# Where ScalarE's gates stand between the roots of a norm, and when the gated branch's preparation begins

## What is computed

```python
u = _rms_norm(h, norm_mix_pre[l])
(a_q, a_k, a_v, b_q, b_k, b_v, b_r, b_g, c_qa, c_kva, c_kr,
 d_q, d_k, d_v, gate_logits) = jnp.split(u @ w_in[l], offsets, axis=-1)
o_a = _diff_attention(...)          # branch a, ends in a norm over each head
o_b = _gla(...)                     # branch b: gated linear attention, ends in a norm over each head
o_c = _mla(...)                     # branch c, begins with norms of its latents
o_d = _window_gqa(...)              # branch d
branches = jnp.stack([o_a, o_b, o_c, o_d], axis=2)
gates = jax.nn.sigmoid(gate_logits.reshape(bsz, T, N_BRANCH, D_MODEL))
merged = jnp.sum(jnp.einsum('btnw,nwd->btnd', branches, w_branch[l]) * gates, axis=2)
h = h + _rms_norm(merged @ w_out[l], norm_mix_post[l])
```

## Time and profile before

| | |
|---|---|
| median of three runs | 2257.65 us (2256.54 to 2262.7) |
| the profiled execution: its time | 2256.57 us |
| its span | 2254.8 us |
| TensorE's granted clock over the span | 0.99 |
| weight chunks (instructions of L1653, and of L2077) | 650 |
| table loads of L1646, L1750, L1758 | 22, 2, 12 |

### The profile page before, as it was taken

One profiled execution on the slowest core, in us unless ns is written; L12 is line 12 of the kernel. 1 busy time (PEld: TensorE's weight loads), 2 busy tenths in 40 slices (PEclk: granted clock), 3 DMA queues, 4 the chain that ended last, 5 costly groups with the idle time before them and its releaser, 6 DMA issues.

```text
span 2254.8 us, 43338 instructions
## 1 busy us (share of the span) xinstructions
PE 2175.6 (96%) x17522; PEld 2088.3 (93%) x17522; DVE 1519.6 (67%) x2614; ACT 1218.1 (54%) x2069; POOL 301.4 (13%) x285
## 2 busy tenths in 40 slices
PE   7989999899999899998999999999999999999998
PEld 6878989799988789897998999989999999989998
DVE  5766676787467566859865665667665665887654
ACT  4565465666446564656655544456444544565443
POOL 1000102100110001120001220001220221132221
PEclk9999999999999999999999999999999999999999
DMA  7333435365543344355554555435555555444553
GB/s 240 108 109 103 143 127 160 117 186 173 175 157 103 113 128 142 122 179 173 185 187 149 188 186 187 149 114 160 187 187 185 182 188 185 156 134 154 185 187 131
DMA packets 97815, 356.61 MB, mean 158 GB/s; under 512 B 10848, under 2 KB 12000, under 8 KB 97488
## 3 DMA queue, kind: packets, MB, share of 16 engines
q1 hardware_dynamic: 95328, 342.47, 46.9%
q0 software_dynamic: 2000, 10.38, 1.7%
q10 hardware_dynamic: 288, 0.99, 0.1%
HBM read 352.68 MB, written 1.12 MB: 157 GB/s over the span
## 4 chain that ended last, share of the span: by engine, by line
PE 85%; DVE 9%; ACT 4%; issue 2%; DMA 0%; POOL 0%; SPq 0%; DVEq 0%; ACTq 0%; POOLq 0%
PE pd L1242 26%; PE pd L1248 25%; PE pd L1245 25%; DVE wlo L2077 2%; ACT whi L1653 1%; DVE xl L2087 1%; PE pt L1347 1%; PE pd L1363 1%; DVE u L2116 1%; DVE h L2123 1%; PE ps L1556 1%; PE ps L1322 1%; PE pd L1469 1%; PE pd L1377 1%; PE ps L1336 0%
## 5 line engine op out<-in xcount | busy, mean ns | idle before, releaser
L1242 PE MATMUL pd<-xh,whi 128*128 128x256 f32 (+2 forms) x3584 | 1054.1, 294 | 24.7 <-issue 10.2
L1245 PE MATMUL pd<-xl,whi 128*128 128x256 f32 (+2 forms) x3584 | 1024.6, 286 | 10.8 <-DVE xl L2087 9.9
L1248 PE MATMUL pd<-xh,wlo 128*128 128x256 f32 (+2 forms) x3584 | 1023.4, 286 | 3.2 <-DVE wlo L2077 3.2
L1653 ACT ACTIVATE whi<-raw 128x1024 fp32r<-128x1024 f32 x650 | 684.9, 1055 | 628.4 <-PE pd L1248 613.2
L2077 DVE TENSOR_TENSOR wlo<-raw,whi 128x1024 fp32r<-128x1024 f32 x650 | 807.8, 1244 | 303.6 <-ACT whi L1653 301.7
L1242 PEld LDWEIGHTS pd<-xh,whi 128*128 128x128 f32 x3584 | 681.8, 190 | 51.9 <-issue 37.9
L1245 PEld LDWEIGHTS pd<-xl,whi 128*128 128x128 f32 x3584 | 680.7, 190 | 18.4 <-DVE xl L2087 14.2
L1248 PEld LDWEIGHTS pd<-xh,wlo 128*128 128x128 f32 x3584 | 682.3, 190 | 5.3 <-DVE wlo L2077 5.1
L1248 PE MATMUL pd<-ah,wlo 128*128 128x256 f32 (+1 forms) x1056 | 298.8, 283 | 0.0
L1245 PE MATMUL pd<-al,whi 128*128 128x256 f32 (+1 forms) x1056 | 297.8, 282 | 0.0
L1242 PE MATMUL pd<-ah,whi 128*128 128x256 f32 (+1 forms) x1056 | 297.5, 282 | 0.0
(11 more groups left out here) (319 smaller groups left out, 2503.9 us busy)
## 6 DMA issues: line engine op xcount, KB each, us to landing
raw<-in_w SPq DMA_DIRECT2D x648, 512.0 KB, 3.5
TA<-scr POOLq DMA_DIRECT2D x2, 1392.0 KB, 9.9
C<-in_c POOLq DMA_DIRECT2D x1, 2432.0 KB, 12.8
TD<-scr POOLq DMA_DIRECT2D x2, 1056.0 KB, 7.9
TD<-scr POOLq DMA_DIRECT2D x2, 768.0 KB, 13.1
h<-in_h SPq DMA_DIRECT2D x4, 272.0 KB, 7.4
out<-u SPq DMA_DIRECT2D x8, 128.0 KB, 1.8
C<-in_c POOLq DMA_DIRECT2D x1, 800.0 KB, 5.5
```

Source lines behind the costliest of these rows:

```text
L1242: e.matmul(out, hi, xh, start=begin, stop=False)
L1245: e.matmul(out, hi, xl, start=False, stop=False)
L1248: last = e.matmul(out, lo, xh, start=False, stop=end)
L1653: e.activation(m.whi[c % NSPL][:, 0:n], m.raw[c % NRAW][:, 0:n], ACT.Copy).then_inc(*self.up("ac_hi", ("hi", c)))
```

## The change

Two things change in the plan's times.

1. `head_norm` and the latents' norm note a stretch (`begin`, `end`) of the plan, from shortly after the first square to behind the last root. When the lists are settled, every "gate" and "silu_tanh" step of ScalarE that falls in such a stretch is put at its end. The preload of the root's set (`table`) moves from ahead of the first square to the stretch's beginning.
2. The four `b_gate` matmuls and all the steps of the gated branch's preparation that are timed from them stand 0.8 chunks later.

```diff
--- before.py
+++ after.py
@@ -149,7 +149,7 @@
         self.holds = {}
         self.n = 0
         self.late = set()
-        self.out_tiles, self.last_early = {}, []
+        self.out_tiles, self.last_early, self.roots = {}, [], []
 
     def now(self):
         return len(self.chunks) + len(self.open) / 8
@@ -234,6 +234,10 @@
             at[stage] = at.get(stage, 0) + len(blocks) * 128 * 128
             for tile, _ in blocks:
                 self.final[tile.key[0], tile.x] = self.final[tile.key[:2]] = c
+
+        for begin, end in self.roots:
+            self.steps["ac"] = [(end if name in ("gate", "silu_tanh") and begin <= t < end else t, n, name, args)
+                                for t, n, name, args in self.steps["ac"]]
         for k in self.steps:
             self.steps[k].sort(key=lambda s: s[:2])
 
@@ -441,7 +445,7 @@
             t += 1.0
         self.head_norm("a", l, t + 6.2)
 
-        t = gk[0].end + 0.8
+        t = gk[0].end + 1.6
         for c in range(4):
             t = self.fit(t, ("pd", ("b_gate", l, c), 0, 0.6))
             self.step("pe", t, "b_gate", l, c)
@@ -489,12 +493,15 @@
             for j in range(a, b):
                 self.step("ac", t + 0.1 * (j - a), "c_sq", l, j)
                 self.step("pe", t + 0.1 * (j - a) + 0.5, "c_ones", l, j)
+            if i == 0:
+                begin = t + 0.7
             self.step("ac", t + 0.8, "c_rs", l, i)
             for j in range(a, b):
                 self.step("dv", t + 1.4, "c_norm", l, i, j)
                 self.step("ac", t + 1.7, "c_hi", l, j)
                 self.step("dv", t + 2.0, "c_lo", l, j)
             t += 0.3
+        self.roots.append((begin, t + 0.55))
         for i in range(2):
             q = qu[4 + i]
             e = self.fit(q.end + 0.05, ("tn", ("pe", l, i), 0, 2.0), ("tn", ("pr", l, i), 1.1, 2.0),
@@ -532,10 +539,12 @@
         self.post_norm(stage, self.now())
 
     def head_norm(self, kind, l, t):
-        self.step("ac", t - 0.01, "table")
         for h in range(4):
             key = ("head", kind, l, h)
             t = self.fit(t, ("sq", key, 0, 0.8), ("pd", key, 0.5, 1.3), ("tn", key, 0.8, 2.0))
+            if h == 0:
+                begin = t + 0.3
+                self.step("ac", begin, "table")
             self.step("ac", t, "head_sq", kind, l, h)
             self.step("pe", t + 0.6, "head_ones", kind, l, h)
             self.step("ac", t + 0.8, "head_rs", kind, l, h)
@@ -543,6 +552,7 @@
             self.step("ac", t + 1.8, "o_hi", kind, l, h)
             self.step("dv", t + 2.1, "o_lo", kind, l, h)
             t += 0.4
+        self.roots.append((begin, t + 0.5))
 
     def bias_tables(self, t):
         self.step("gp", t - 20, "load_btab")
```

## The result

| | before | after |
|---|---|---|
| median of five runs | 2258.05 us (2256.54 to 2262.7) | 2235.69 us (2232.16 to 2236.36) |
| the profiled execution | 2256.57 us | 2235.22 us |
| its span | 2254.8 us | 2233.4 us |
| ratio of the times | | 0.9898, interval 0.9885 to 0.991 |

22.4 us less by the medians and 21.35 by the profiled executions; the forecast was 19.3 less. So the change is faster, inside the range, and by a little more than expected. Lines of the code have moved by 10 (L1386 is now L1396, L1347 is L1357, L2077 is L2087).

What follows compares the result with a forecast made beforehand. TensorE, busy 96% of the span, was taken as the bound. Gates (14.7 us) plus preparation (4.6 us) made 19.3 us off 2256.57, so 2237.3, put at 2238; own range 2231 to 2244, 8-in-10 range 2230 to 2248.

Steps and rivals of the forecast that it cites:

- What bounds the kernel: TensorE, busy 96% of the span; fewer ScalarE loads only count where TensorE stops waiting or running at half clock in the mixers.
- Part 1, branch a's norm: Fewer table loads between the roots end TensorE's idling and half clock: 6.98 us in layer 0, 6.34 in layer 1.
- part 1: Gates and their table loads moved behind the last root in the norms: 14.7 us gained, of it 3.8 by the clock.
- Part 1, branch b's norm: Four loads go in the norm of branch b's heads; TensorE's idle time of 0.95 and 1.03 us goes: 1.98.
- Part 2, layer 0: Preparation 0.8 chunks later: P<-P on VectorE comes 1.4 us earlier, so TensorE waits 1.4 us less; ends 0 and 4.25.
- The clock's share: Layer 0's preparation: half of the 1.68 us lost at half clock behind the wait at 124.11 is gained, 0.8 us.
- Part 2, layer 1: Preparation: 1.1 us at 740.30, as BR goes ahead of the KB products, plus 1.3 on the way to P<-P: 2.4.
- Sum: Gates 14.7 plus preparation 4.6: 19.3 us off the profiled 2256.57, giving 2237.3; forecast put at 2238.
- A wait behind the last root: Rival: TensorE waits out one load and two gates, 2.14 us, at all four norms; about 2247 us; chance 0.10.
- The preparation did not lose: Rival: the moved preparation meets a fuller VectorE and loses some 3 to 5 us instead of gaining 4.6; 2246; chance 0.10.
- the forecast's own signs of being wrong: A TensorE wait for KT, KB or KN, or half clock in a mixer where it had been full.
- The chain through five engines: Rival: preparation's chain, passing between engines five times, comes 14 us late and becomes the bound; 2264 us; chance 0.04.

Runs made afterwards that it cites:

- (4): Kernel with the gates moved and the preparation unmoved, plus eight table loads put back ahead of branch a's first two heads' roots over both layers: 2252.34 us.
- after, again: The changed kernel run once more with nothing changed, for a second profile: median 2234.15 us, profiled 2235.78 us.
- preparation only: The kernel before with only the gated branch's preparation 0.8 chunks later, gates and tables between the roots as before: 2253.59 us, ratio 0.9976.
- the gates alone: The changed kernel with the gated branch's preparation put back to its old place, so only gates and root tables move: 2237.56 us, ratio 0.9902.
- run 6: The changed kernel with VectorE's two products of QD 2.3 chunks later, behind the last head's P<-P: 2231.12 us.
- run 9: The changed kernel with VectorE's two products of QD 3.7 chunks later, also behind the last copy of PT: 2228.09 us, ratio to before 0.9859.
- run 11: The changed kernel with one wait added on POOL, so its products of KI start only after VectorE's products of KB: 2229.71 us.
- run 7: As run 6, and P<-P of heads 1 and 3 of branch a also stands 0.2 chunks earlier on VectorE: 2232.38 us.

## Why the prediction was right, step by step

**What bounds the kernel.** Right. Sixteen loads fewer on ScalarE were worth what TensorE stopped waiting, and the places were those named.

**Part 1, branch a's norm.** Right in mechanism, somewhat small: forecast 6.98 and 6.34, less 0.3 each for waiting left over; measured 7.48 and 7.33. The waiting left over was 0.07. That is 2.1 us of the 4.7 by which part 1 came out too small; I did not trace these start by start, but the stops here were priced by idle time, too, with the fault that the next part shows. Putting the loads back (4) brought the waits back, and the gates' place alone did not.

**Part 1, branch b's norm.** This term of the sum was mis-sized: forecast 0.95 + 1.03 = 1.98, measured 2.07 + 2.56 = 4.6. It was read as idle time of windows, length less busy. TensorE's rows there, in the kernel before:

```profile
207.11 0.29 PE L1245 MATMUL pd<-xl,whi 128*128 128x272 f32 x1
207.24 0.29 PE L1248 MATMUL pd<-xh,wlo 128*128 128x272 f32 x1
207.61 0.73 PE L1386 MATMUL pd<-sq,C 128*128 128x272 f32 x2
...
209.76 0.28 PE L1248 MATMUL pd<-ch,wlo 128*128 128x272 f32 x1
210.25 0.40 PE L1242 MATMUL pd<-ch,whi 128*128 128x272 f32 x1 [0.20 <-ACT tb L1663]
...
211.00 0.28 PE L1248 MATMUL pd<-ch,wlo 128*128 128x272 f32 x1
211.94 0.39 PE L1242 MATMUL pd<-xh,whi 128*128 128x272 f32 x1 [0.66 <-ACT tb L1910]
```

In an undisturbed row matmuls start every 0.125 us (207.11, 207.24), but each is shown 0.29 long. A matmul that starts 0.37 after the one before has lost 0.24, and the rows show 0.08 of idle time; 0.49 apart is 0.36 lost (0.20 shown), 0.94 apart is 0.81 lost (0.66 shown). The three together have lost 1.4 by their starts, where the rows show 0.95. So the window hides 0.17 us at each stop. Matched start by start, before against after, these three stops make up 1.25 of the 2.07 and the matmuls next behind them 0.2 more. The other 0.6 went at 209.41, 214.93 and 217.06, about 0.2 each: there the rows show no idle time at all, and the last two lie outside the window of 204 to 214 besides.

**Part 2, layer 0.** The 1.4 us of less waiting were right in size: TensorE turned the last `P` 1.8 us (after, again) and 2.05 us (preparation only) earlier, of which 0.3 and 0.5 were there before the preparation began. VectorE's idle times of 2.42 and 1.13 went, too. But the way to TensorE was other than told. The wait at that turn was forecast to shrink from 3.27 to 2.9; it is 3.19, and what went were two small waits ahead of it, by the starts 0.7 us at 109.53 and 0.6 at 113.52, both earlier than VectorE's idle time at 115.31, from which the forecast took its 1.1:

```profile
109.53 0.70 PE L1322 MATMUL ps<-AK,AQ 64*96 64x272 f32 x4 [0.55 <-DVE st L2273]
...
113.52 1.64 PE L1363 MATMUL pd<-PT,AV 96*128 96x272 f32 x6 [0.44 <-DVE PT L2337]
```

The clock's share failed: the forecast took half of 1.68 as gained, but the fall behind this wait was there in both executions and in the preparation alone, at 1.7 us or twice that.

**Part 2, layer 1.** Forecast 2.4, measured 2.28 and 2.29 where the clock stayed, but by other terms. The 1.09 us at `PT` went, and 0.72 came at the turn of `KB`. The wait for the last `P`, which was to shrink, grew from 1.27 to 2.19; small stops ahead of it had given 2.4 us. In the profiled execution of after a fall of the clock, 1.7 us, followed this wait; in the second execution the wait is the same and none followed. One mechanism there was not foreseen: `P<-P,st` took 2.07 us beside POOL's products instead of 0.89.

**Sum.** 19.4 for part 1 where 14.7 was forecast, and about 4.1 for part 2 in the execution whose clock in the preparations was as before, where 3.8 was forecast without the clock and 4.6 with it; together 23.5. In the table the four norms give 19.4 in both executions of the changed kernel. The two preparations give 0.1 in the first and 4.1 in the second; the other rows, where the change moves nothing, give 1.8 in the first and take 2.7 in the second. So the first came to 2.1 below 23.5 and the second to 2.7 below it, mostly by falls of the clock in different places. The forecast's nearness in the sum owes something to that, and that is luck: part 1 was 4.7 too small, and falls of the clock elsewhere took back about half of it.

**The rivals.** A wait behind the last root did not come: the row of load and two gates begins at 149.12 and TensorE's idle time there is 0.07. The preparation did not lose as such, though in layer 0 of the profiled execution it looks so, by its clock. Of the forecast's own signs of being wrong one did come, half clock in a mixer where it had been full: at 92 and at 727 in the first execution, at 170 in the second. The chain through five engines did not become the bound: no run shows a wait for `KB`; the turn of `KB` waits for the copy of `PT` alone. The rule of the Trainium skill (ScalarE: Activation LUTs, What ACT_TABLE_LOAD costs), by which every switch would cost 2.66 us, is not what these rows show: in the changed kernel a load of 1.28 at 149.12 is followed by the gate at 150.41, 0.01 later, and at 141.17 by the next square at 142.46.

## What to carry to other kernels

Price a stop of TensorE by the starts of its instructions, not by the window's idle time: at each stop the shown length of a pipelined matmul hides about 0.17 us, and the shortest stops don't show; together that was more than half of one term here. When an engine with long instructions stands between two tightly packed ones, look for steps in its queue whose result is used much later, and put them behind the ones that are waited for, together with whatever the neighbouring engine does that slows it. And before a gain that is lost again is put down to a queue, compare the falls of the clock in the two executions: in the preparation alone it was the clock.

## What the runs showed of the hardware that was not expected

**What falls of the clock cost.** I went through PEclk of every trace and summed (1 - PEclk) times the length, leaving out the last microseconds of each execution. Each fall took 1.7 us of clock, or twice that, or three times in branch a's norm in the preparation alone and with the loads put back: ten entries in the kernel before, 20.5 us in all. The changed kernel's first profile has 20.5 as well, its second 17.0, the gates alone 17.0, run 6 13.6, run 9 11.9. So between the two profiled executions compared here nothing was gained by the clock in all, though in the norms the half clock went: others, at 92 and 727 among them, came in their place. One fall is in all eight profiles that have a wait of 3.19 to 3.28 us at the last `P` of layer 0, behind that wait; others come and go between executions of the same program (at 92, at 170, at 727). Behind a wait of 1.72 us there was one (run 11), behind 1.64, 1.66, 1.67 and 1.15 none; behind 2.13 one (run 7), behind 2.02 none. Each of these is one profile. One or two falls more or less are the size of the spread between runs of one kernel, 3 to 4 us. The Trainium skill (TensorE: Matmul & The Clock Gate, Part 1) says that the gate watches out of step with the program. The two executions of one program, with falls in different places, agree with that.

**POOL and VectorE take turns.** In experiment 11's rows POOL's second product, 1.33 us in the kernel before (half of the 2.67 in the earlier trace rows), took 2.35 from 114.27, and VectorE's difference beside it 1.85 in place of 1.22. VectorE's ends at 115.40, and POOL's 1.22 later at 116.62, as if it had stood until then; and the products of `QD`, begun at 115.68, are 0.8 us longer than alone. The Trainium skill (SBUF — State Buffer, Who interferes with whom) says that the two engines' shared ports are an exclusive lock, and that a VectorE instruction with two inputs in SBUF takes it against a POOL instruction that reads there; the rows agree. In layer 1 it cost most: three `P<-P,st`, 0.89 us alone, took 2.07.
